# Modulation weights multiplied as plain float32, and five of their twelve groups moved into the ramps of two scans

## The reference

```python
s_lat, s_ctx = silu(c), silu(c_ctx)              # two vectors of 1024
mod_l = split(s_lat @ w_mod + b_mod, 6)          # w_mod: 1024 x 6144
mod_c = split(s_ctx @ w_mod + b_mod, 6)
h_lat = rms_norm(x_lat, g1) * (1 + mod_l[1]) + mod_l[0]     # 512 tokens
h_ctx = rms_norm(x_ctx, g1) * (1 + mod_c[1]) + mod_c[0]     # 256 tokens
y = gdn_mixer(h_ctx, h_lat)     # projection, 5-tap convolution, gated delta scan, output gate, projection
x_lat = x_lat + mod_l[2] * y
h_lat = rms_norm(x_lat, g2) * (1 + mod_l[4]) + mod_l[3]
x_lat = x_lat + mod_l[5] * conv_glu(h_lat)
```

## Time and profile before

| | |
|---|---|
| median of three runs | 3799.03 us (3799.02 to 3799.54) |
| span of the profiled execution | 3798.2 us; no time of its own is given beside it, so the span stands for it, 0.8 us below the median |
| TensorE busy | 3626.4 us, 95% of the span |
| VectorE, ScalarE, GpSimd busy | 1927.2, 1525.7, 862.4 us |
| constants: issued, landed | 6.70 us, 16.6 us later |
| first projection starts | 62.39 us |
| scan 0 starts, scan 1 starts | 244.35, 549.29 us |
| output gate starts | 735.41 us |

### The profile page before, as it was taken

How to read it: one execution, slowest core, us unless ns; L and a number is a source line. 1 busy time by engine, 2 the same in 40 slices (tenths; PEclk the granted TensorE clock), 3 DMA queues, 4 the chain that set the end, 5 groups by cost and what they waited for, 6 DMA issues and landing times.

```text
span 3798.2 us, 59716 instructions
## 1 busy us (share of the span) xinstructions
PE 3626.4 (95%) x25058; PEld 2920.6 (77%) x25058; DVE 1927.2 (51%) x2901; ACT 1525.7 (40%) x2602; POOL 862.4 (23%) x847
## 2 busy tenths in 40 slices
PE   6999899999999999989999999999999899999999
PEld 3679779878887667768887888875778688878887
DVE  5666566655355656653344443446565523454343
ACT  5534333333233456643234322234664522343222
POOL 1123323312020324431101111113354211002020
PEclk7999999999999999999999999999999999999999
DMA  6310120133232111112333223220211132322232
GB/s 245 124 45 3 36 55 4 41 102 99 95 100 83 45 56 57 62 39 84 100 100 100 95 94 100 94 72 23 78 62 62 40 98 97 118 82 94 95 99 89
DMA packets 81970, 300.79 MB, mean 79 GB/s; under 512 B 8872, under 2 KB 10024, under 8 KB 81064
## 3 DMA queue, kind: packets, MB, share of 16 engines
q1 hardware_dynamic: 80672, 294.90, 23.4%
q10 hardware_dynamic: 1032, 2.10, 0.5%
HBM read 292.76 MB, written 4.19 MB: 78 GB/s over the span
## 4 chain that ended last, share of the span: by engine, by line
PE 72%; DVE 11%; ACT 6%; issue 5%; POOL 4%; DMA 1%; SPq 0%; DVEq 0%; POOLq 0%; ACTq 0%
PE ps L208 71%; DVE ac L247 2%; DVE wlo L239 2%; DVE he L247 1%; ACT whi L227 1%; PE ps L213 1%; DVE hc L2532 1%; ACT ha L227 1%; POOL p L243 1%; ACT L227 1%; DVE ha L239 1%; DVE ws L247 1%; ACT sg L227 1%; ACT wp L228 1%; DVE sml L2000 1%
## 5 line engine op out<-in xcount | busy, mean ns | idle before, releaser
L239 DVE TENSOR_TENSOR wlo<-wraw,whi 128x1024 fp32r<-128x1024 f32 x537 | 691.5, 1293 | 732.5 <-ACT whi L227 731.7
L208 PE MATMUL ps<-hh,whi 128*128 128x512 f32 x1856 | 737.5, 397 | 7.6 <-ACT p L228 1.9
L208 PE MATMUL ps<-hh,wlo 128*128 128x512 f32 x1856 | 728.7, 393 | 0.0
L208 PE MATMUL ps<-hl,whi 128*128 128x512 f32 x1856 | 728.4, 392 | 0.0
L227 ACT ACTIVATE whi<-wraw 128x1024 fp32r<-128x1024 f32 x537 | 559.6, 1050 | 209.5 <-PE ps L208 169.7
L208 PEld LDWEIGHTS ps<-hh,whi 128*128 128x128 f32 x1856 | 352.1, 190 | 92.1 <-ACT hh L227 6.5
L208 PEld LDWEIGHTS ps<-hh,wlo 128*128 128x128 f32 x1856 | 351.8, 190 | 74.6
L208 PEld LDWEIGHTS ps<-hl,whi 128*128 128x128 f32 x1856 | 352.0, 190 | 71.6
L208 PE MATMUL ps<-u,u 64*64 64x64 f32 (+1 forms) x6016 | 222.1, 225 | 16.5 <-DVE u L239 9.7
L208 PEld LDWEIGHTS ps<-u,u 64*64 64x64 f32 x6016 | 202.7, 134 | 34.7 <-DVE u L239 13.4
L208 PE MATMUL ps<-gh,wlo 128*128 128x512 f32 x528 | 205.4, 389 | 0.0
(11 more groups left out here) (416 smaller groups left out, 6873.4 us busy)
## 6 DMA issues: line engine op xcount, KB each, us to landing
wraw<-weights SPq DMA_DIRECT2D x537, 512.0 KB, 3.3
x<-xT SPq DMA_DIRECT2D x1, 2048.0 KB, 11.9
bias_lines<-ln ACTq DMA_DIRECT2D x1, 2048.0 KB
x<-xT SPq DMA_DIRECT2D x4, 512.0 KB, 5.3
xmf<-memT SPq DMA_DIRECT2D x2, 1024.0 KB, 5.4
out<-x SPq DMA_DIRECT2D x4, 512.0 KB, 2.6
bias<-bias_lines SPq DMA_DIRECT2D x1, 1536.0 KB, 8.0
con<-consts SPq DMA_DIRECT2D x1, 1379.0 KB, 16.6
```

The lines of the kernel that those rows point to most:

```text
L208: self.last, self.open = self.e.matmul(out, lhsT, rhs, start=start, stop=stop, skip_group_check=skip), True
L239: return self.e.tensor_tensor(out, a, b, op)
```

## The change

Modulation is multiplied in plain float32 straight from the loaded blocks, with no halves. The stationary operand `svec` is 128x32 for each k (two vectors, thirty zero columns), and even and odd k go to PSUM partitions 0 to 31 and 32 to 63; `pe_mod_turn` adds the two parts through a wider selection table. Blocks of modulation are marked plain; feeds skip them, and a plain block never shares with a split one. Groups 4, 5, 6 stay in chunks 0, now in steps 1, 3, 5. Groups 7, 8, 9 go into scan 0 and 10, 11 into scan 1, two k (one block) ahead of each phase number in `MOD_AT`, their turns three phases behind. The deeper feeds are gone. The ramp's idle products are gone. The ring of eight buffers ends at block 16. Scan 0 feeds the first block of chunks 1 at phase 190; scan 1 has no such feed.

```diff
-EARLY = 48
+EARLY = 16
+MOD_CHUNKS = {1: 4, 3: 5, 5: 6}
+MOD_SCANS = ((7, 8, 9), (10, 11))
+MOD_AT = (1, 2, 3, 4, 6, 7, 8, 9, 10, 11, 12, 13)
-        self.shl = self.sb("shl", m + 160, [128, 8, 4], F32R)
+        self.svec = self.sb("svec", m + 896, [128, 8, 32])
 def act_feed(self, *group, ahead=1):          # dve_feed alike
         while act.fed <= last:
             b = act.fed
+            act.fed += 1
+            if b in self.plain:
+                continue
...
+    def take_plain(self, key, n):
+        if self.off + n > BL or self.blk not in self.plain:
+            self.next_block()
+            self.plain.add(self.blk)
+            self.pe.wait_ge(self.arrived(self.blk))
+        w = self.raw[self.slot(self.blk)][:, self.off:self.off + n]
...
 def pe_mod(self, g, ks=ks8, hold=False):
-        pe.wait_ge(self.act.at("shi"), self.dve.at("slo"))
+        pe.wait_ge(self.dve.at("svec"))
         for k in ks:
-            hi, lo = self.take(self.mod_key(g, k), 512)
-            pe.mm(b[0:4, :], self.shl[:, k, :], hi, k == 0, False)
-            pe.mm(b[0:4, :], self.shl[:, k, :], lo, False, k == 7)
+            w, o = self.take_plain(self.mod_key(g, k), 512), 32 * (k % 2)
+            pe.mm(b[o:o + 32, :], self.svec[:, k, :], w, k < 2, k > 5)
+            self.used_up()
 def act_mod(self, g, rows):
-        self.act_feed("mod", g, ahead=2)
-        act.cp(row, self.ps["mod", g][0:4, :]).then_inc(act("mrow", g), 1)
+        act.cp(row, self.ps["mod", g][0:64, :]).then_inc(act("mrow", g), 1)
 def act_chunks(self, hg):                     # dve_chunks alike
-                K.act_feed("c", *z, ahead=1 if new is None else 2)
+                K.act_feed("c", *z)
 def mod_step(self, hg, c):
-        return (4 + c if hg == 0 and c < 8 else None), (3 + c if hg == 0 and 1 <= c < 9 else None)
+        return (MOD_CHUNKS.get(c), MOD_CHUNKS.get(c - 1)) if hg == 0 else (None, None)
 def pe_scan(self, hg):
+        slots, turns = K.mod_slots(hg), K.mod_ends(hg, 3)
+        for n, (s, ph) in enumerate(gdn_order()):
+            if n in turns:
+                K.pe_mod_turn(turns[n], K.mrow2)
+            if n in slots:
+                g, i = slots[n]
+                K.pe_mod(g, (2 * i, 2 * i + 1), hold=True)
...
-                if s == 0:
-                    K.pe_keep(3, "ramp", hg)
 def act_scan(self, hg):                       # dve_scan alike, dve_mod five phases behind
+            if n in rows:
+                K.act_mod(rows[n], K.mrow2)
+            if hg == 0 and n == 190:
+                K.act_feed("c", 1, "q", 0, ahead=0)
```

More of the change, by code:

```diff
@@ L64, in const_table @@
     add("half2", np.stack([i < 64, i >= 64], 1))
-    add("both2", np.stack([(i < 4) & (i % 2 == v) for v in range(2)], 1))
+    add("both2", np.stack([(i < 64) & (i % 32 == v) for v in range(2)], 1))
     add("mhalf", np.full((128, 1), -0.5))
@@ L396, in __init__ @@
         self.wd = self.line = None
-        self.block_of, self.nblk = {}, 0
+        self.block_of, self.nblk, self.plain = {}, 0, set()
         self.layout()
@@ L500, in layout @@
         self.barow = self.sb("barow", U + 6456, [32, 768])
-        self.mrow = self.ring("mrow", [self.sb("mrow", W + 12288 + 512 * i, [4, 512]) for i in range(2)])
-        self.mrow2 = self.ring("mrow2", [self.sb("mrow", U + 5432 + 512 * i, [4, 512]) for i in range(2)],
+        self.mrow = self.ring("mrow", [self.sb("mrow", W + 12288 + 512 * i, [64, 512]) for i in range(2)])
+        self.mrow2 = self.ring("mrow2", [self.sb("mrow", U + 7680 + 512 * i, [64, 512]) for i in range(2)],
                                lambda: K.ended("norm1"))
@@ L682, in dve_feed @@
             b = dve.fed
+            dve.fed += 1
+            if b in self.plain:
+                continue
             dve.wait_ge(self.arrived(b), act.at("whi", b))
@@ L701, in take, with next_block, used_up @@
         return hi, lo
+    def next_block(self):
+        if self.blk >= 0 and not self.spent:
+            self.pe.mark("used", self.blk)
+        self.blk += 1
+        self.off, self.spent = 0, False
+    def take_plain(self, key, n):
+        if self.off + n > BL or self.blk not in self.plain:
+            self.next_block()
+            self.plain.add(self.blk)
+            self.pe.wait_ge(self.arrived(self.blk))
+        w = self.raw[self.slot(self.blk)][:, self.off:self.off + n]
+        self.plan.append((self.blk, self.off, key, n))
+        self.off += n
+        return w
+    def used_up(self):
+        if self.off == BL and not self.spent:
+            self.pe.mark("used", self.blk)
+            self.spent = True
     def proj(self, group, keys, rhs):
@@ L886, in pe_mod @@
             self.block_of["mod", g] = self.blk
+            if hold:
+                self.ps.drop("mod", g)
     def pe_mod_turn(self, g, rows):
@@ L893, in pe_mod_turn @@
         for c in range(4):
-            pe.mm(b[:, 2 * c:2 * c + 2], rows[(g,)][:, c * 128:c * 128 + 128], self.con("both2")[0:4, :])
+            pe.mm(b[:, 2 * c:2 * c + 2], rows[(g,)][:, c * 128:c * 128 + 128], self.con("both2")[0:64, :])
         pe.mark("modt", g)
@@ L950, in act_start @@
         K.act_mod(0, K.mrow)
-        K.act_feed("mod", 1, ahead=0)
+        K.act_feed("c", 0, "q", 0)
         K.act_shift(lat, range(4), K.x, K.HHI, 0)
@@ L965, in dve_start @@
         K, dve = self, self.dve
+        dve.e.memset(K.svec, 0.0).then_inc(dve("svec0"), 1)
         dve.wait_ge(K.loaded("vecs"))
@@ L1120, in mod_step, with mod_slots, mod_ends @@
     def mod_step(self, hg, c):
-        return (4 + c if hg == 0 and c < 8 else None), (3 + c if hg == 0 and 1 <= c < 9 else None)
+        return (MOD_CHUNKS.get(c), MOD_CHUNKS.get(c - 1)) if hg == 0 else (None, None)
+    def mod_slots(self, hg):
+        at = {}
+        for n, g in enumerate(MOD_SCANS[hg]):
+            for i in range(4):
+                at[MOD_AT[4 * n + i]] = (g, i)
+        return at
+    def mod_ends(self, hg, after):
+        return {MOD_AT[4 * n + 3] + after: g for n, g in enumerate(MOD_SCANS[hg])}
     def pe_chunks(self, hg):
@@ L1244, in dve_chunks @@
                 new, old = K.mod_step(hg, c)
-                K.dve_feed("c", *z, ahead=1 if new is None else 2)
+                K.dve_feed("c", *z)
                 if old is not None:
                     K.dve_mod(old)
-                if new is not None:
-                    K.dve_feed("mod", new)
                 c += 1
@@ L1485, in act_scan @@
         H = lambda ap, h: ap[:, h * 128:h * 128 + 128]
-        for s, ph in gdn_order():
+        rows = K.mod_ends(hg, 1)
+        for n, (s, ph) in enumerate(gdn_order()):
+            if n in rows:
+                K.act_mod(rows[n], K.mrow2)
+            if hg == 0 and n == 190:
+                K.act_feed("c", 1, "q", 0, ahead=0)
             par, lat, (XY, BA, EP, EQ, R) = K.unit(s)
@@ L1532, in dve_scan @@
         H = lambda ap, h: ap[:, h * 128:h * 128 + 128]
-        for s, ph in gdn_order():
+        turned = K.mod_ends(hg, 5)
+        for n, (s, ph) in enumerate(gdn_order()):
+            if n in turned:
+                K.dve_mod(turned[n])
+            if hg == 0 and n == 190:
+                K.dve_feed("c", 1, "q", 0, ahead=0)
             par, lat, (XY, BA, EP, EQ, R) = K.unit(s)
@@ L3284, in tensor @@
         K.pe.begin(e)
-        K.blk, K.off, K.plan = -1, BL, []
+        K.blk, K.off, K.plan, K.spent, K.plain = -1, BL, [], True, set()
         K.pe_start()
```

37 lines of the change are left out of this document (11 added, 26 removed).

## The result

The changed kernel takes 3850.38 us (median of four, 3848.61 to 3854.54) against 3799.03: ratio 1.0135, 95% interval 1.012 to 1.0149. The forecast was 3805, range 3788 to 3824, so it missed by 45 us on the slow side. The profiled execution, the slowest of the four, spans 3852.7 us, 54.5 more than that of before.

A forecast was written before the change was run, and what follows sets the result against it. It took TensorE to bound the scans, and waits for split blocks the time before. Terms -18.7, -12.9, +3, +16.7, +9.3, +8.0 sum to +5.4 us on the span of 3798.2: about 3805, range 3788 to 3824.

The forecast's parts named there:

- Block edges: Groups of projections now begin on block edges: 0.3 us charged for each of about ten steps, +3 (0 to 10).
- a rival with a chance of 0.08: Edges cost the full 0.8 us a step, the half block's shift 3 us in later stages: 3813, chance 0.08.
- Start: Up to q0's convolution: first projection at 50.4 us, 12.0 earlier, at the high clock, convolution waiting less; -18.7 us together.
- Chunks 0: Sigmoid of q0 to that of k3: steps without a group shrink, steps behind one wait for splits; 110.3 against 123.2, -12.9 us.
- Scan 0: Ramp slots, turns and an extra `wlo` at phase 190 (0.7) lengthen the scan, nothing given back behind the ramp: +16.7 us.
- scan 1: First slot at the low clock, second hidden, six more slots and two turns lengthen the scan: +9.3 us.
- Output gate: First block split only behind scan 1: 5.3 us of idle TensorE and 2.7 for the low clock, +8.0.
- Tiles without overlap: Rival: 32-column tiles don't overlap; start +5.3, chunks +4, twenty slots +8: 3822, chance 0.20.
- The clock did not stay high: Faster rival: TensorE keeps 2.4 GHz across the new waits, without 14.9 us of low clock: 3790, chance 0.12.
- not near 214: Sign of being right: scan 0 starts near 214 us and lasts 17 us longer.
- named as a sign of being wrong: Sign in the scans' ramps: slots that cost less than 1 us each.
- Another of these signs: Sign of being wrong: TensorE waits for blocks to land, with only four buffers ahead in chunks 0.

The follow-up runs named there:

- e4_whi_wait: Changed kernel, but ScalarE's feed waits for the last split block in the same `whi` buffer, no longer for a plain one; 3844.92 us, ratio 1.012.
- e1_half_og: Changed kernel with the output gate's first weight block entered at column 512, so later block edges fall as in the kernel before; 3805.05 us, ratio 1.0016.
- e9_feed_mid: Changed kernel with scan 0's split of the first block of chunks 1 moved from phase 190 to phases 96 and 104; 3850.51 us, ratio 1.013.
- e3_og_feed: Changed kernel with the output gate's first block split at phase 190 of scan 1; 3848.46 us, ratio 1.0129.
- e7_serial: From e1_half_og, all eight k of a modulation group go to partitions 0 to 31, no tiles side by side; 3836.57 us, ratio 1.0093.

## Why the prediction was wrong, step by step

**Block edges: the step that failed.** The forecast saw the shift and priced it: `wlo` 0.8 late in a k step, 0.3 charged for about ten steps, +3, and 3 us for all later stages in a rival with a chance of 0.08. The size of one late block was right (0.86 measured), and so was chunks 1 (+3.4). But the count stopped at the chunks. In the FFN TensorE is the bound, so the whole 0.86 is paid, 21 times, and the stages behind lose 17.6 more, with waits for `wlo` of up to 3.3 us. 36 of the 49 us by which the span missed the forecast's sum (54.5 against 5.4) are this. What should have been asked is, for each stage up to the end of the program, how far ahead its feed splits and whether TensorE is the bound there, and not only for the steps near the change.

**Start, -18.7 forecast.** The first projection came 2.4 us earlier, not 12.0. Two things were missed. One is the clock: it was given as low only for turn 2 and the half group behind it, but in this execution it stayed at 1.2 GHz to 42.09 with TensorE busy throughout:

```profile
22.49:42.09 19.60, 19.60 (x73) 13.32 (x73) 0.74 (x5) 3.15 (x9) 3.76 (x5) 0.50 0.76 299
```

So the scaling of x began at 42.20, 5.4 us behind the forecast's 36.8. From there to the projection it took 17.8 us instead of 13.6. In this lies the other thing, the feed's wait for blocks that never held its buffer, 2.4 to 3.6 us (e4_whi_wait). Up to the sigmoid of q0, 71.92 against 79.52, the start gave 7.6.

**Chunks 0, -12.9 forecast.** From the sigmoid of q0 to that of k3 the profiled execution shows 116.4 us, that is -6.7; the execution of e1_half_og, the same program there, 113.1, -10.0. The waits were as forecast: 8.96 ahead of q2, 4.59 ahead of the gates' group, 5.93 ahead of k2.

```profile
87.01 0.76 PE L211 MATMUL ps<-hhi,whi 128*128 128x512 f32 x1 [8.96 <-DVE wlo L242]
...
113.56 0.61 PE L211 MATMUL ps<-hhi,whi 128*32 128x512 f32 x1 [4.59 <-DVE wlo L242]
```

The three steps that hold them take 70.0 us, forecast 70.2. The miss is in the four others, whose chain was priced too low: 46.4 us in this execution and 42.0 in e1_half_og's, where 40.1 were forecast; k0 to k1 alone takes 15.5 and 12.7, forecast 12.0. The granted clock from 130 to 160 us was 0.81 in the one and 0.90 in the other; why it differed is open.

**Scan 0 +12.0 (forecast +16.7), scan 1 +6.3 (+9.3).** The mechanism was right, nothing is given back behind the ramp; the slot was mis-sized, 0.98 us instead of 1.4. The split at phase 190 erred the other way, 2.5 us (e9_feed_mid) where 0.7 was charged. The forecast let only the second record of one product run beside the next; the rows above show two products in the time of one. The clock at scan 0's head was 1.00, where 0.70 was carried over from the earlier trace rows; at scan 1's it was 0.50.

**Output gate +8.0: right.** It starts 5.39 us behind the scan, and the stretch to the FFN is 8.5 longer; e3_og_feed shows that an earlier split takes its price inside the scan.

**The rivals.** Tiles without overlap would have cost 31 us (e7_serial), where the rival said 17; they do overlap. The clock did not stay high. The side, slower, had the largest chance, 0.51, and came out; but its reason is one to which 0.08 was given, with 3 us where the runs show 36. With the phase restored the change measures 1.0016, near the forecast of +5.4 us; that is partly luck: in e1_half_og's execution scan 0 starts at 228.03, 14 us later than forecast, while the scans cost 9 less than forecast and the stages behind the FFN stretch ran 6 shorter than before, within the 8 us over which they scatter with the same phase.

**The signs.** Scan 0 started at 232.4 us, not near 214. A ramp slot at 0.98 us is just under the 1 us that was named as a sign of being wrong. Another of these signs showed faintly: TensorE waited for blocks to land, three times and 1.8 us in all, in chunks 0.

The Trainium skill, "TensorEngine Tiling (Array Packing)", section Key Properties, says that different tiles can execute in parallel and that changing the tiling mode drains TensorE. The runs agree with the first: 0.99 us a slot against 1.84. On the second they put a bound: two tiles at two records of 0.43 each leave 0.13 of the slot's 0.99 for everything else, and e7_serial's 1.84 leaves 0.13 as well.

## What to carry to other kernels

Where weights come as one stream in fixed blocks, the phase at which a group enters a block is a state that lasts to the end of the program: whoever changes the number of columns taken early on must read the wait for the split block in every stage behind, up to the last. It can be 0.62 us at every second group, as in the FFN here, or 3.3 us at a single one. A feed ahead is a number of blocks, and its worth changes with the phase. And a free-looking slot in an in-order queue, ahead of the sigmoid or inside a scan, is free only if the next user of that engine isn't the chain of the stage.

## What the runs showed of the hardware

Two 128x32 float32 products in different column tiles take the time of one, 0.86 us at 2.4 GHz, and 0.13 more: one product leaves two records of 0.43 each, and in one tile the same two take 1.84 us (e7_serial). So plain float32 in two tiles costs 0.49 us a slice in a slot of two, about as much as the two fp32r products of before (0.46). The start of the same program ran at different clocks in different executions: the sums of squares in the changed kernel's profile

```profile
27.81 6.99 PE L211 MATMUL ps<-con,hsq 128*128 128x1 f32 x32
```

and in e9_feed_mid's, where the first projection came 4.4 us earlier:

```profile
27.37 4.24 PE L211 MATMUL ps<-con,hsq 128*128 128x1 f32 x32
```

Why the clock rose in the one and not in the other is open.
